# First six matmul jobs on the unscaled input, squares in pairs, convolution taps from chunk 6

## The reference, cut to what matters

```python
h = rms_norm(x, norm1_g[l])            # x * rsqrt(mean(x*x) + 1e-6) * g
z = h @ w_in[l]
glu_in, q, k, v, gate_logits = jnp.split(z, SPLITS, axis=-1)
a_val, a_gate = jnp.split(glu_in, 2, axis=-1)
a = a_val * jax.nn.sigmoid(a_gate)
a = causal_depthwise_conv(a, conv_w[l], conv_b[l])
a = jax.nn.silu(rms_norm(a, conv_norm_g[l]))
```

## Time and profile before

| | us |
|---|---|
| median of 3 runs | 875.8 |
| lowest, highest | 875.26, 878.95 |
| the profiled execution | 875.62 |
| its span, first to last instruction | 873.8 |
| PE busy | 843.5 |
| DVE busy | 652.3 |
| ACT busy | 555.2 |
| POOL busy | 228.7 |

### The profile page before, as it was taken

How to read it: one execution, slowest core, us unless ns; L and a number is a source line. 1 busy time by engine, 2 the same in 40 slices (tenths; PEclk the granted TensorE clock), 3 DMA queues, 4 the chain that set the end, 5 groups by cost and what they waited for, 6 DMA issues and landing times.

```text
span 873.8 us, 16525 instructions
## 1 busy us (share of the span) xinstructions
PE 843.5 (97%) x5984; PEld 788.8 (90%) x5984; DVE 652.3 (75%) x1158; ACT 555.2 (64%) x1009; POOL 228.7 (26%) x252
## 2 busy tenths in 40 slices
PE   4999999999999999999999999999999999999996
PEld 3998989999998999999888889999998888888885
DVE  6989999895779898787766858847589866556552
ACT  5777979986746676666555586466646666555441
POOL 2258633331322053333111100010022142222111
PEclk9999999999999999999999999999999999999999
DMA  5756464444566466555547444445346466555741
GB/s 207 222 189 199 144 188 143 132 138 125 165 194 192 122 199 203 180 186 178 197 168 218 140 170 143 121 122 169 117 140 185 146 211 191 178 188 168 225 135 49
DMA packets 42304, 146.11 MB, mean 167 GB/s; under 512 B 4704, under 2 KB 7024, under 8 KB 42224
## 3 DMA queue, kind: packets, MB, share of 16 engines
q1 hardware_dynamic: 41472, 143.67, 52.6%
q10 hardware_dynamic: 752, 1.39, 0.5%
HBM read 144.00 MB, written 1.05 MB: 166 GB/s over the span
## 4 chain that ended last, share of the span: by engine, by line
PE 82%; DVE 11%; issue 4%; ACT 3%; DMA 1%; POOL 0%; DVEq 0%; ACTq 0%
PE px L518 20%; PE px L522 14%; PE px L523 13%; PE px L524 13%; PE px L519 10%; DVE wlo L1327 4%; DVE px L1381 2%; PE px L561 1%; PE px L583 1%; PE px L528 1%; PE px L529 1%; PE px L530 1%; PE px L718 1%; DVE hx L1344 1%; PE px L584 1%
## 5 line engine op out<-in xcount | busy, mean ns | idle before, releaser
L1327 DVE TENSOR_TENSOR wlo<-raw,whi 128x1024 fp32r<-128x1024 f32 x267 | 334.3, 1259 | 28.6 <-ACT whi L857 28.5
L857 ACT ACTIVATE whi<-raw 128x1024 fp32r<-128x1024 f32 x267 | 280.1, 1052 | 59.4 <-PE px L519 29.1
L522 PE MATMUL px<-hx,whi 128*128 128x256 f32 x1072 | 310.9, 290 | 4.8 <-DVE hx L1344 3.1
L523 PE MATMUL px<-hx,whi 128*128 128x256 f32 x1072 | 304.1, 284 | 0.0
L524 PE MATMUL px<-hx,wlo 128*128 128x256 f32 x1072 | 304.0, 284 | 0.0
L522 PEld LDWEIGHTS px<-hx,whi 128*128 128x128 f32 x1072 | 206.1, 192 | 8.0 <-DVE hx L1344 4.2
L523 PEld LDWEIGHTS px<-hx,whi 128*128 128x128 f32 x1072 | 206.5, 193 | 0.4
L524 PEld LDWEIGHTS px<-hx,wlo 128*128 128x128 f32 x1072 | 206.3, 192 | 0.0
L518 PE MATMUL px<-fx,whi 128*128 128x512 f32 x330 | 115.6, 393 | 0.0
L518 PE MATMUL px<-hx,whi 128*128 128x512 f32 x320 | 113.4, 399 | 0.8 <-DVE wlo L1327 0.5
L1892 POOL TENSOR_TENSOR CA<-CA,ct 128x256 f32<-128x256 f32 x90 | 79.2, 880 | 112.5 <-ACT ct L924 56.3
(11 more groups left out here) (298 smaller groups left out, 1286.7 us busy)
## 6 DMA issues: line engine op xcount, KB each, us to landing
raw<-ws SPq DMA_DIRECT2D x267, 512.0 KB, 3.6
tb<-tabs SPq DMA_DIRECT2D x16, 128.0 KB, 2.3
out<-X SPq DMA_DIRECT2D x4, 256.0 KB, 2.5
X<-xs SPq DMA_DIRECT2D x1, 512.0 KB, 4.9
X<-xs ACTq DMA_DIRECT2D x1, 512.0 KB, 5.0
vc<-vecs ACTq DMA_DIRECT2D x1, 320.0 KB, 6.8
msk<-lmask ACTq DMA_DIRECT2D x1, 256.0 KB, 2.8
ug<-pos ACTq DMA_DIRECT2D x1, 128.0 KB, 3.9
```

What stands on the lines that cost most here:

```text
L522: e.matmul(b[:, 0:S], H, xh, start=first, stop=False)
L523: e.matmul(b[:, 0:S], H, xl, start=False, stop=False)
L857: e.activation(whi[:, n % NSL, :], raw[:, n % NRAW, :], ACT.Copy).then_inc(s_hi, 1)
L1327: e.tensor_tensor(wlo[:, n % NSL, :], raw[:, n % NRAW, :], whi[:, n % NSL, :], ALU.subtract).then_inc(s_lo, 1)
```

## The change

1. **Input.** `x` comes in four transfers of two tiles, all on SyncE's queue, with the first two chunks of weights in halves among them; the vectors come in two parts, the first (the norm's gain and epsilon, 9 columns) on ScalarE's queue.
2. **Six jobs without 1 / rms.** ScalarE and VectorE split `x * gain` straight into high and low parts (`ax`), and the first six jobs (`ag` and `av` 0 to 2, `EARLY` = 3) use these. The sum for 1 / rms runs on TensorE behind the first two jobs. VectorE multiplies the six results by 1 / rms (`early`), ScalarE takes the tanh from SBUF (`early_gate`), and VectorE forms the product (`early_gated`). `ag` takes its banks from `FEW`, `av` from `SMALL` in these six; the sum goes to bank 7. The tiles of `hx` are made between, for the seventh job on.
3. **Halves.** The high and low parts of chunks 0 and 1 are made half a chunk at a time.
4. **Squares** are taken two tiles at a time, four instructions in place of eight, and added in three instructions in place of six.
5. **TensorE** runs 16 matmuls of ones by ones first (`WARM`), whose result nobody reads.
6. **Taps** begin at chunk 6 for the first three tiles at once, with quotas on VectorE of 2.2 a chunk up to chunk 11, 3.2 up to 23, 2.6 up to 33 as before, and 3.7 from there; before 2.9, 2.9, 2.6 and 3.5.

By the plan VectorE's 155 taps stand so:

| chunks | before | after |
|---|---|---|
| up to 23 | 63 | 52 |
| 24 to 33 | 26 | 26 |
| 34 to 46 | 46 | 47 |
| 47 to 51 | 17 | 19 |
| 52 to 54 | 3 | 11 |

Tile 7's taps, which are alone on VectorE at the end, are the last 20 before and the last 30 after.

The diff, cut to its core:

```diff
+FIRST_VECS = 9
+HALVED = 2
+
+WARM = 16
+EARLY = 3
...
-        quota = (2.9 if c < 24 else 2.6 if c < 34 else 3.5, 2.0 if c < 34 else 1.8)
+        quota = (2.2 if c < 12 else 3.2 if c < 24 else 2.6 if c < 34 else 3.7, 2.0 if c < 34 else 1.8)
         for n, side in enumerate((2, 1)):
             if chains[n]:
                 owed[n] += quota[n]
             owed[n] -= some(n, side, int(owed[n]), c)
-        if c < 16 and c % 2:
-            i = c // 2
-            chains[i in CONV_G].append([i, 0])
+        if c < 16 and c % 2 and c >= 2 * EARLY - 1:
+            for i in range(EARLY) if c < 2 * EARLY else (c // 2,):
+                chains[i in CONV_G].append([i, 0])
...
+        LOW = {c: (s_lo, c + 1 + min(c + 1, HALVED)) for c in range(n_chunks)}
+
+        HI = [c + 1 + min(c + 1, HALVED) for c in range(n_chunks)]
...
+            return (s_ci, i + 1) if i < EARLY else BANK[("av", i), 0]
...
+                    if c < HALVED and o in (0, CW // 2):
+                        e.wait_ge(s_lo, 2 * c + 1 + (o > 0))
...
+                if inst == "n1":
+                    e.wait_ge(s_add, 3)
+                    e.matmul(b[:, 0:S], ones[:, :], sqa[:, 0, :], start=True, stop=False, skip_group_check=True)
+                    e.matmul(b[:, 0:S], ones[:, :], sqa[:, 1, :], start=False, stop=True, skip_group_check=True).then_inc(
+                        s_sum, 1)
+                    return
...
-            sums("n1")
-            for i in range(KD):
-                job(("ag", i), HX, normed("n1") if i == 0 else None, rings=(FEW,))
+            def first_scaled(k):
+                e.wait_ge(s_xgl, k + 1)
+
+
+            e.wait_ge(s_con, 1)
+            for _ in range(WARM):
+                e.matmul(px[VALUES[0]][:, 0:P], ones[:, :], ones[:, :], start=True, stop=True, skip_group_check=True)
+            for i in range(EARLY):
+                job(("ag", i), AX, first_scaled if i == 0 else None, rings=(FEW,))
+                job(("av", i), AX, rings=(SMALL,))
+                if i == 0:
+                    sums("n1", VALUES)
+            for i in range(EARLY, KD):
+                job(("ag", i), HX, normed("n1") if i == EARLY else None, rings=(FEW,))
                 job(("av", i), HX, rings=(FEW,))
...
+            def half_high(n, h):
+                e.wait_ge(s_raw[n] if h else s_half[n], 16)
+                e.activation(whi[:, n, half(h)], raw[:, n, half(h)], ACT.Copy).then_inc(s_hi, 1)
...
+            e.dma_start(vc[:, 0:FIRST_VECS], vecs[:, 0:FIRST_VECS]).then_inc(s_vg, 16)
             e.preload_act_table_set(LOG)
-            e.dma_start(X[:, 0:4, :], xv[:, 0:4, :]).then_inc(s_x[0], 16)
-            e.dma_start(vc[:, :], vecs).then_inc(s_vc, 16)
-            e.wait_ge(s_x[0], 16)
+            e.wait_ge(s_vg, 16)
             for i in range(KD):
-                if i == 4:
-                    e.wait_ge(s_x[1], 16)
-                square("n1", i, X[:, i, :])
-            highs(1)
-            e.wait_ge(s_vc, 16)
+                if i % 2 == 0:
+                    e.wait_ge(s_x[i // 2], 16)
+                e.activation(ax[:, i, 0, :], X[:, i, :], ACT.Copy, scale=vec("norm1_g", i)).then_inc(s_xgh, 1)
+                if i == 3:
+                    half_high(0, 0)
+            half_high(0, 1)
+            half_high(1, 0)
+            half_high(1, 1)
+            e.activation(sqa[:, :, :], X[:, 0:2, :], ACT.Square).then_inc(s_sq, 1)
+            for i in range(2, KD, 2):
+                e.activation(sq[:, i - 2:i, :], X[:, i:i + 2, :], ACT.Square).then_inc(s_sq, 1)
+            highs(3)
             rms("n1", D)
-            high_tiles("n1", KD, hx)
+
+            def early_gate(i):
+                e.wait_ge(*BANK[("ag", i), 0])
+                e.activation(sg[:, i, :], sg[:, i, :], ACT.Tanh, scale=0.5).then_inc(s_eg, 1)
+
+            def first_high(i):
+                e.wait_ge(s_nt, i + 1)
+                e.activation(hx[:, i, 0, :], sq[:, nt_slot("n1", i), :], ACT.Copy).then_inc(s_nhi, 1)
+
+            highs(4)
+            for i in range(2):
+                first_high(i)
+            early_gate(0)
+            first_high(2)
+            highs(5)
+            for i in (3, 4):
+                first_high(i)
+            early_gate(1)
+            highs(6)
+            for i in (5, 6, 7):
+                first_high(i)
+            early_gate(2)
+            highs(7)
...
+            def half_low(n, h):
+                e.wait_ge(s_hi, 2 * n + h + 1)
+                e.tensor_tensor(wlo[:, n, half(h)], raw[:, n, half(h)], whi[:, n, half(h)], ALU.subtract).then_inc(s_lo, 1)
...
-            for i in range(1, KD - 1):
-                e.wait_ge(s_sq, FROM["sq"]["n1"] + i + 1)
-                if i > 1:
-                    e.wait_ge(s_add, FROM["add"]["n1"] + i - 1)
-                e.tensor_tensor(sqa[:, 0, :], sqa[:, 0, :], sq[:, sq_slot("n1", i), :], ALU.add).then_inc(s_add, 1)
-            lows(1)
+            e.wait_ge(s_vg, 16)
+            for i in range(KD):
+                e.wait_ge(s_xgh, i + 1)
+                e.scalar_tensor_tensor(out=ax[:, i, 1, :], in0=X[:, i, :], scalar=vec("norm1_g", i), in1=ax[:, i, 0, :],
+                                       op0=ALU.mult, op1=ALU.subtract).then_inc(s_xgl, 1)
+                if i == 3:
+                    half_low(0, 0)
+            half_low(0, 1)
+            half_low(1, 0)
+            half_low(1, 1)
+            for i in range(3):
+                e.wait_ge(s_sq, i + 2)
+                if i:
+                    e.wait_ge(s_add, i)
+                e.tensor_tensor(sqa[:, :, :], sqa[:, :, :], sq[:, 2 * i:2 * i + 2, :], ALU.add).then_inc(s_add, 1)
             e.wait_ge(s_vc, 16)
             e.tensor_scalar(hb[:, :], vc[:, V["gate_b"]:V["gate_b"] + 16], 0.5, None, ALU.mult).then_inc(s_cst, 1)
             e.tensor_scalar(cw5[:, :], vc[:, V["conv_w"]:V["conv_w"] + 248], 0.5, None, ALU.mult).then_inc(s_cst, 1)
             e.tensor_scalar(cg5[:, :], vc[:, V["conv_norm_g"]:V["conv_norm_g"] + 8], 0.5, None, ALU.mult).then_inc(s_cst, 1)
             e.tensor_scalar(qg8[:, :], vec("qg"), -0.125, None, ALU.mult).then_inc(s_cst, 1)
-            norm("n1", X, "norm1_g", hx)
+            lows(3)
+
+            def early(key, to):
+
+                e.wait_ge(s_mm, ENDS[key])
+                e.tensor_tensor(to, px_of[key, 0][:, 0:S], rst[:, 0, 0:S], ALU.mult).then_inc(BANK[key, 0][0], 1)
+
+            def early_gated(i):
+                e.wait_ge(s_eg, i + 1)
+                e.wait_ge(*BANK[("av", i), 0])
+                e.scalar_tensor_tensor(out=CI[:, i, 30:], in0=sg[:, i, :], scalar=1.0, in1=CI[:, i, 30:], op0=ALU.add,
+                                       op1=ALU.mult).then_inc(s_ci, 1)
+
+            def first_tiles(scales, low_parts):
+                for i in scales:
+                    scaled("n1", i, X[:, i, :], "norm1_g")
+                for i in low_parts:
+                    low_tile("n1", i, hx)
+
+            e.wait_ge(s_rms, 1)
+            early(("ag", 0), sg[:, 0, :])
+            early(("av", 0), CI[:, 0, 30:])
+            first_tiles((0, 1), ())
+            first_tiles((2,), (0, 1))
+            lows(4)
+            early(("ag", 1), sg[:, 1, :])
+            early_gated(0)
+            first_tiles((3, 4), (2, 3))
+            lows(5)
+            early(("av", 1), CI[:, 1, 30:])
+            first_tiles((5,), (4,))
+            early_gated(1)
+            early(("ag", 2), sg[:, 2, :])
+            lows(6)
+            first_tiles((6, 7), (5, 6, 7))
+            lows(7)
+            early(("av", 2), CI[:, 2, 30:])
+            early_gated(2)
...
-            e.dma_start(X[:, 4:8, :], xv[:, 4:8, :]).then_inc(s_x[1], 16)
+            def tiles(i):
+                e.dma_start(X[:, 2 * i:2 * i + 2, :], xv[i]).then_inc(s_x[i], 16)
+
+            def half_load(n, h):
+                e.dma_start(raw[:, n, half(h)], ws[n][:, half(h)]).then_inc(s_raw[n] if h else s_half[n], 16)
+
+            tiles(0)
+            tiles(1)
+            half_load(0, 0)
+            tiles(2)
+            tiles(3)
+            half_load(0, 1)
+            half_load(1, 0)
+            half_load(1, 1)
+            loads(2)
+            e.dma_start(vc[:, FIRST_VECS:], vecs[:, FIRST_VECS:]).then_inc(s_vc, 16)
```

46 lines of the change are left out of this document (25 added, 21 removed).

## The result

The changed kernel takes 870.25 us in the median of five executions (868.08 to 872.03); five of the kernel before, on the same chip, have a median of 877.35 (875.26 to 878.95). The ratio is 0.9927, with a 95% interval of 0.9904 to 0.9949. The profiled execution took 872.03 us, its span is 870.2.

A forecast was written before the change was run, and what follows sets the result against it. TensorE was taken as the bound, with VectorE the bound from 89 to 144 us. The terms summed as 875.6 - 8.4 + 0.4 + 0.4 = 868.0 us, range 865.6 to 871.8.

The forecast's parts named there:

- term of 8.4 us: Start of the kernel: the eighth job, `av` 3, begins at 28.9 us against 37.35, a gain of 8.4 us.
- rival of the lower level: First jobs: TensorE at the lower clock level, 2.4 us more to the sum, 870.3 us in all; chance 0.12.
- more is won: Start: the ones end at 6 us and all behind moves forward, about 866.5 us, or 865; chance 0.07.
- Late transfers: Start: input transfers land as late as before, VectorE 2.5 us late up to chunk 3, 869.8 us; chance 0.08.
- VectorE's added work at 0: Up to chunk 24: 4.7 us of added VectorE work is offset by fewer taps and idle time, costing 0.
- The slower rival: Whole kernel: VectorE is the bound all the way and its idle time takes no work, 883 us; chance 0.03.
- Chunks 24 to 46 at +0.4: Chunks 24 to 46: 73 VectorE taps instead of 72 cost 0.4 us more.
- the waits of the earlier trace stay: Chunks 24 to 46: TensorE's waits for VectorE, 3.2 us in front of attention scores, stay as before.
- The late taps at +0.4: Chunks 47 to 54: taps moved late mostly fit in VectorE's gaps and cost 0.4 us, within 0 to 5.6.
- The rival of taps that do not hide: Late chunks: all 11 moved taps lie on the path, 5.2 us more, 873.2 us; chance 0.10.

The follow-up runs named there:

- e3: The changed kernel with the second head's scores in a bank of their own (bank 7) instead of the ring of three; 869.99 us, ratio 0.9933.
- e2: The changed kernel without its 16 matmuls of ones at the start; 871.31 us, ratio 0.9948.
- e1: The changed kernel run again without any edit, as the measure for the others; 870.23 us, ratio 0.9928.
- e7: The kernel before with 14 matmuls of ones ahead of the second head's scores; 875.97 us, ratio 1.0004.
- e6: The kernel before with only the new plan of taps; 875.68 us, ratio 0.9996.
- e11: The changed kernel with VectorE's tap quotas 2.6 up to chunk 11 and 3.5 from chunk 34, in place of 2.2 and 3.7; 868.89 us, ratio 0.9909.

## Why the prediction was right, and where its terms were off

The forecast was 868.0 in 865.6 to 871.8; measured were 870.25 and 870.23. The forecast's own range (866.8 to 869.3) is missed by 1 us. The gain was to be 7.6 us; by the ratio it is 6.4 (4.5 to 8.4).

**The start.** The mechanism is as argued: first job at 7.45 (7.5 forecast), the sum at 13.96 (13.3), the first product with 1 / rms at 15.98 (15.2), `av` 3 at 29.77 (28.9). The term of 8.4 us measured 7.6 and 7.3 in the two traces, 7.1 in the lowest of the same start (e3). Three durations were mis-sized. The gain vector landed 2.9 us after its issue and let ScalarE start at 3.70, not 3.25; the input's transfers landed 3.7 us after their issue in the median, the halves of chunks 5.0, where I had taken 2.5 and a rate, so that ScalarE could take up the first half chunk only at 5.94 and not from 4.5 on. And I took ScalarE's tiles 0.30 us apart from squares of the same shape; the copy with a gain for each channel has this row:

```profile
L945 ACT ACTIVATE ax<-X,vc 128x256 fp32r<-128x256 f32 x8 | 3.4, 498 | 1.2 <-DMA vc<-vecs 1.2
```

Four of them took 1.71 us, so they follow each other at 0.40. The trace of before had rows for it, which I did not use: the same copy with a gain in a later norm, and the copy without one.

```profile
L1076 ACT ACTIVATE hx<-X,vc 128x256 fp32r<-128x256 f32 x24 | 12.2, 510 | 28.1 <-DVE X L1518 28.1
L884 ACT ACTIVATE hx<-sq 128x256 fp32r<-128x256 f32 x32 | 11.3, 406 | 3.3 <-DVE sq L1339 3.3
```

Together this puts the half chunk's low part at 6.61, done at 7.30 where I had 6.05. That the first job still began at 7.45, where 7.5 was forecast, is luck: I had it wait for the ones, to 7.5, and they ended at 6.35; it waited for the weights, which came 1.25 us later than I had them. The lag then shows as two waits, 0.60 us at the fifth step (9.68) and 0.47 at `av` 3 (29.77), where ScalarE's high part of chunk 7 stands behind tiles and a tanh; that queue I had named, and given up to 0.6.

**The ones** ended at 6.35 (7.5 forecast; 11 at 0.5 and 5 at 0.25 us from 0.95 would be 7.7), having reached the upper level on the way, and the gap of 1.1 us up to the first job did not bring it down. The rival of the lower level (870.3) did not happen. Its price was too high: e2, which is that rival made, lost 0.3 to 0.8 us at `av` 3 and not 2.4. The likely reason is that TensorE waits for VectorE there anyhow; no run tests that apart. The rival "more is won" had its condition nearly met (an end at 6) and not its gain, again because the weights came last. **Late transfers** did come, though smaller than in that rival: it would have had VectorE at work at 6.57, and it began at 4.32.

**VectorE's added work at 0** holds up to chunk 24. VectorE still waits for ScalarE there, 2.2 us, against the 1.8 of the earlier trace rows:

```profile
82.32 1.23 DVE L1400 TENSOR_TENSOR wlo<-raw,whi 128x1024 fp32r<-128x1024 f32 x1 [2.19 <-ACT whi L899]
```

The slower rival (VectorE the bound all the way, 883) is refuted by this row and by TensorE, busy for all of 30 to 78.

**Chunks 24 to 46 at +0.4** was too small, and "the waits of the earlier trace rows stay" was the step that failed. To the second head's scores the loss is 0.6 us (7.6 to 7.0; 0.8 in e1). But the wait grew from 2.15 to 2.64 and 2.90 us, and behind it the clock fell in the changed kernel's first trace, which costs 1.5 us more; that a wait can bring such a second price was not in my sum. Not all of it is the change's, since by its mean granted clock (e7) before pays it in many executions too. At the sixth head 1.0 us was won, at the eighth 0.8 lost, which e6 traces to the plan and e11 to its quotas. In sum the stretch costs 0.7 us without the fall (e1: 7.3 to 6.6) and 1.9 with it (7.6 to 5.7).

**The late taps at +0.4** cost nothing. From the ninth head to the last the difference stays at 5.7, and the last head's output moved with it, from 215.32 to 209.65, with VectorE idle ahead of it:

```profile
203.89 0.48 DVE L1500 SCALAR_TENSOR_TENSOR CA<-CI,cw,px 128x256 f32<-128x256 f32 x1
...
209.65 0.42 DVE L1557 TENSOR_TENSOR ax<-px,ax 128x256 fp32r<-128x256 f32 x1 [4.14 <-ACT ax L1086]
```

Of the 6.1 us gap 4.1 are left: the last four taps fitted in it, as argued. From the ninth head on the heads follow each other at 4.50 us, as forecast. The rival of taps that do not hide (873.2) fell, and its place in the range's upper part was not used.

So the terms as measured are -7.3 to -7.6, +0.7 or +1.9, and 0, which is 5.7 to 6.6 us won at the ninth head where 8.0 was forecast there; from there on executions of one program differ by more than the rest of the sum. The time lies in the range because the mechanism of the start is right; it lies above the forecast because of 0.8 to 1.1 us too much at the start and 0.3 to 1.5 too little in chunks 24 to 46, less the 0.4 put down for the late taps.
